# FFN steps of a two-network kernel: two weight blocks of a pair split by one operation per engine

## The reference, cut to what matters

```
def swiglu(h, w1, w3, w2):
    return (jax.nn.silu(h @ w1) * (h @ w3)) @ w2

x = x + 0.5 * m[:, 0, 2][:, None] * swiglu(adaln_in(x, norm_g[l, 0], m, 0),
                                           ffn_w1[l, 0], ffn_w3[l, 0], ffn_w2[l, 0])
```

## Time and profile before

| | |
|---|---|
| median of 3 runs | 1666.9 us (1659.82 to 1667.51) |
| profiled execution | 1665.64 us |
| its span, first to last instruction | 1663.8 us |
| PE busy | 1467.2 us (88%) |
| DVE busy | 1384.0 us (83%) |
| ACT busy | 985.6 us (59%) |
| mean granted TensorE clock | 0.942 of full |

### The profile page before, as it was taken

The page is one execution under the profiler, slowest core; times in us unless marked ns, Lnnn a source line. Parts: engine busy times, 40 slices in busy tenths (PEclk is TensorE's granted clock), DMA queues, the critical chain, the costliest instruction groups (busy, mean ns, idle before and its releaser), DMA issues.

```text
span 1663.8 us, 27728 instructions
## 1 busy us (share of the span) xinstructions
PE 1467.2 (88%) x11160; PEld 1392.3 (84%) x11160; DVE 1384.0 (83%) x2275; ACT 985.6 (59%) x1643; POOL 79.3 (5%) x152
## 2 busy tenths in 40 slices
PE   5897786798978887988899999899999999988997
PEld 4897775687978886867899999888899899868997
DVE  7597957799999998886888988796788888787986
ACT  4354554565566455654666766556666766676765
POOL 0012110001110110000000000000000000000000
PEclk9698988999999999999999999898999999999999
DMA  9499945569986996426697787444677677534783
GB/s 384 150 406 351 411 152 190 214 226 361 353 308 226 402 404 260 139 90 267 218 322 270 244 278 275 143 150 152 250 280 276 232 267 271 210 115 185 275 274 127
DMA packets 84973, 420.30 MB, mean 253 GB/s; under 512 B 9364, under 2 KB 9796, under 8 KB 58095
## 3 DMA queue, kind: packets, MB, share of 16 engines
q1 hardware_dynamic: 64478, 343.48, 56.9%
q0 software_dynamic: 20368, 75.06, 11.9%
HBM read 417.37 MB, written 1.13 MB: 252 GB/s over the span
## 4 chain that ended last, share of the span: by engine, by line
PE 42%; DVE 7%; ACT 2%; issue 1%; DVEq 0%
PE pw L628 14%; PE pw L629 13%; PE acc L628 6%; PE acc L629 6%; DVE low_p L1965 2%; DVE low_d L1965 1%; PE acc L938 1%; PE pw L896 1%; DVE h_lo L1818 1%; DVE x L2012 0%; PE acc L918 0%; ACT hi_p L1453 0%; ACT h_hi L1363 0%; DVE prob L2154 0%; DVE KR L2154 0%
## 5 line engine op out<-in xcount | busy, mean ns | idle before, releaser
L628 PE MATMUL pw<-h_hi,hi_p 128*128 128x256 f32 x2928 | 740.8, 291 | 38.1 <-DVE low_p L1965 28.0
L629 PE MATMUL pw<-h_lo,low_p 128*128 128x256 f32 x2928 | 729.7, 288 | 0.0
L628 PEld LDWEIGHTS pw<-h_hi,hi_p 128*128 128x128 f32 x2928 | 576.0, 197 | 58.7 <-DVE low_p L1965 28.9
L629 PEld LDWEIGHTS pw<-h_lo,low_p 128*128 128x128 f32 x2928 | 576.5, 197 | 0.4 <-issue 0.2
L1965 DVE SCALAR_TENSOR_TENSOR low_p<-hi_p,land_p 128x1024 fp32r<-128x1024 f32 x418 | 507.6, 1222 | 44.7 <-ACT hi_p L1453 44.5
L1453 ACT ACTIVATE hi_p<-land_p 128x1024 fp32r<-128x1024 f32 x418 | 434.4, 1048 | 74.4 <-DMA land_p<-stream 74.4
L628 PE MATMUL acc<-a_hi,hi_d 128*128 128x256 f32 x1376 | 354.5, 293 | 66.3 <-DVE low_d L1965 60.0
L629 PE MATMUL acc<-a_lo,low_d 128*128 128x256 f32 x1376 | 350.5, 291 | 0.0
L628 PEld LDWEIGHTS acc<-a_hi,hi_d 128*128 128x128 f32 x1376 | 274.1, 199 | 74.1 <-issue 67.5
L629 PEld LDWEIGHTS acc<-a_lo,low_d 128*128 128x128 f32 x1376 | 274.7, 200 | 0.0
L1965 DVE SCALAR_TENSOR_TENSOR low_d<-hi_d,land_d 128x1024 fp32r<-128x1024 f32 x205 | 249.7, 1219 | 5.9 <-ACT hi_d L1453 5.8
(11 more groups left out here) (356 smaller groups left out, 1757.7 us busy)
## 6 DMA issues: line engine op xcount, KB each, us to landing
land_p<-stream SPq DMA_DIRECT2D x207, 1024.0 KB, 5.1
land_d<-stream SPq DMA_DIRECT2D x209, 512.0 KB, 5.5
modw<-wmod POOLq DMA_DIRECT2D x116, 512.0 KB, 8.3
biasT<-wmod POOLq DMA_DIRECT2D x12, 512.0 KB, 4.8
biasT<-bias_rows POOLq DMA_DIRECT2D x3, 1536.0 KB, 10.6
modw<-wmod SPq DMA_DIRECT2D x8, 512.0 KB, 11.2
biasT<-wmod SPq DMA_DIRECT2D x8, 512.0 KB, 14.6
biasT<-bias_rows POOLq DMA_DIRECT2D x1, 3072.0 KB, 13.5
```

The source lines that it names most:

```text
L628: mm(o, lhs[0], rhs[0], start=start, stop=False, skip_group_check=True)
L629: return mm(o, lhs[1], rhs[1], start=False, stop=stop, skip_group_check=True)
```

## The change

In the FFN steps the two blocks of a pair are split by one operation per engine, over both blocks (128 x 2048), where there were two operations of 128 x 1024. On ACT both now come after `a_hi`, followed by the third block. On DVE the low part of step j-1's third block moves behind the gate, to where block 0's low part was, and the low part of the pair comes after `a_lo`. DVE uses the wide operation in smooth steps only, ACT in all steps. Where the pair has one block, or lies behind the end of the stream, the old operations are used.

```diff
@@ ACT
+            def pair_high(group):
+
+                if len(group) < 2 or group[0][0] >= NT:
+                    split_high(group)
+                    return
+                t = group[0][0]
+                assert SPLITS[high[0]:high[0] + 2] == group
+                high[0] += 2
+                act.wait_ge(land_load[t % NPAIR], 16 * (t // NPAIR + 1))
+                fn(hi_p[:, t % NPAIR], land_p[:, t % NPAIR], ACT.Copy, scale=1.0 / TWICE).then_inc(hi_ready, 2)
+
...
-                between = STEPS[i, j][0:1] if smooth(i, j) else []
-                split_high(between)
                 act.wait_ge(gated_ready, f * NFF + j + 1)
                 fn(a_hi[0:r, j % (LAG + 1), :], act_in[0:r, j % 2, :], ACT.Copy, scale=ONCE).then_inc(a_hi_ready, 1)
                 if i == j == 0:
                     hidden_plain(range(KD))
                 if j or not (deferred(i) or i in RAW):
-                    split_high(STEPS[i, j][len(between):])
+                    pair_high(STEPS[i, j][:-1])
+                    split_high(STEPS[i, j][-1:])
@@ DVE
+            def pair_low(group):
+
+                if len(group) < 2 or group[0][0] >= NT:
+                    split_low(group)
+                    return
+                t = group[0][0]
+                assert SPLITS[low[0]:low[0] + 2] == group
+                low[0] += 2
+                dve.wait_ge(hi_ready, SPLIT_NO[t, 1])
+                v.scalar_tensor_tensor(low_p[:, t % NPAIR], hi_p[:, t % NPAIR], -ONCE, land_p[:, t % NPAIR], ALU.mult, ALU.add).then_inc(lo_ready, 2)
+
...
-                    if smooth(i, j) and smooth(i, j - 1):
-                        split_low(STEPS[i, j - 1][-1:])
                     dve.wait_ge(silu_done, f0 + j + 1)
...
                     v.tensor_tensor(act_in[0:r, j % 2, :], sig[0:r, j % 2, :], up_half, ALU.mult).then_inc(gated_ready, 1)
-                    if smooth(i, j):
-                        split_low(STEPS[i, j][0:1])
+                    if smooth(i, j) and smooth(i, j - 1):
+                        split_low(STEPS[i, j - 1][-1:])
                     dve.wait_ge(a_hi_ready, f0 + j + 1)
...
                     if smooth(i, j):
-                        split_low(STEPS[i, j][1:-1])
+                        pair_low(STEPS[i, j][:-1])
```

## The result

The changed kernel takes 1763.82 us (median of 4 runs, 1760.63 to 1767.33); the kernel before took 1667.2 beside it (1659.82 to 1668.12). The ratio is 1.059, with a 95% interval of 1.0553 to 1.0627. The forecast was 1750, in a range of 1727 to 1780. The profiled execution of after took 1767.33 us; against the span of before its span is 101.7 us longer, where the working had added 84.3.

The account below looks back on a forecast made before the run. The prediction took DVE to bound FFNs 0, 2 and 3 and PE the late ones; a closed chain would set longer steps. Stage losses summed to 84.3 us, so 1665.6 + 84.3 = 1750 us, range 1727 to 1780.

Parts of the forecast that it names:

- The closed chain: Gate, a_hi, pair's high part, low part: 4.90 us in FFNs 0, 2, 3; with scaled and silu 6.08 in late FFNs.
- The step: FFNs 0, 2, 3 with two modulation blocks: 7.20 us against 6.42; FFNs 6, 8, 9, 11: 6.08 against 5.76.
- ACT's saving is worth nothing by itself: Wide high part on ACT takes 1.88 us against 1.99 for two; no gain, as ACT is never the bound.
- By stage: Added us: FFN 0 10, FFN 2 13.7, FFN 3 15.8, FFN 5 2, FFNs 6, 8, 9 35.1 together, FFN 11 7.7.
- FFN 0: Adds 13.3 us in 17 steps, 1 in steps 1 and 2, 1.9 at the end, less 6 given back: 10.
- land earlier relative to their use: Transfers: SP's order unchanged and loads start on PE's progress, so they come earlier relative to use; no size given.
- FFN 5: Mean step of 5.4 us stays below PE's 5.76, so only the ends cost: 2 us.
- A: Rival: PE stays at 5.76 us per step in FFNs 6, 8, 9, 11; 1727 us in all; chance 0.06.
- B: Rival: PE's clock falls from 0.95 to 0.86 in three FFNs, 10 us each; 1780 us; chance 0.10.
- C: Rival: pair's high part is ready when DVE comes, only the 0.08 us saving counts; 1662 us; chance 0.02.
- D: Rival: the change doesn't do what it says in the 157 steps; given no chance of its own.
- the bounds of 1740 and 1772: Lower: FFN 0 gets back all 9.4 us, durations 0.05 shorter; upper: wide operations take 1.99 and 2.36 us.

Follow-up runs that it names:

- The first experiment: Changed kernel's order on both engines, but each pair split by two 1024-column operations instead of one of 2048; 1672.12 us, ratio 1.0043.
- e6_first_ffns: The change in FFNs 0, 2, 3 and 5 only, FFNs 6, 8, 9 and 11 as in the kernel before; 1714.96 us, ratio 1.0296.
- e8_flat_low: Changed kernel with the wide low part written over one flat row of 2048 columns instead of 2 x 1024; 1765.19 us, ratio 1.0597.
- e1_narrow: The first experiment: the changed kernel's order with 1024-column operations on both engines; 1672.12 us.
- e7_mixed: Kernel before, with wide operations in steps 3 to 19 of FFNs 0, 2, 3 only, high part ahead of the gate wait; 1667.62 us, ratio 1.0005.

## Why the prediction was right, point by point

**The mechanism: right.** The closed chain from the gate over `a_hi` and the pair's high part to its low part sets the step in FFNs 0, 2 and 3, and scaled and silu join it in FFNs 6, 8, 9 and 11. The kernel with the same order and narrow operations shows that the width makes the chain this long (1672 against 1764), and the one with ACT in the old order that ACT's order is needed for it too (1686). The Trainium skill (Perfetto Trace Analysis, Optimizing Scalar/DVE Operations) ties breaking instructions up to Scalar and Vector engines that aren't saturated but cause bubbles on others, a condition that the prediction left out. The first experiment agrees: in the changed kernel DVE was busy for 78% of the span. Of the same section's sentence that grouping can improve throughput if the engine is saturated, the runs show 0.08 us per step where no engine waits, and nothing in the kernel's time.

**The step.** 7.27 to 7.28 against 7.20, and 6.16 to 6.17 against 6.08. Two terms were small: the handover 0.10 instead of 0.04, and the wide high part 1.90 instead of 1.88. The wide low part was right at 2.29, with the next instruction after 2.21. The sentence that ACT's saving is worth nothing by itself doesn't fit this chain, which ACT's operation is part of: with ACT narrow the kernel took 9.6 us more. 0.08 over 17 + 14 + 18 + 60 + 19 = 128 steps is 10 us of the 17.4 by which the sum fell short.

**By stage,** by the updates of x at the end of each. FFN 2 lost 14.7 (13.7 predicted), FFN 3 14.1 (15.8), FFN 6 14.2, FFN 8 13.6 and FFN 9 13.5 (11.7 each), FFN 11 10.9 (7.7). In FFNs 6, 8 and 9 the longer steps are most of the difference, 1.6 us in each; in FFN 6 one step also took 6.92, since PE had waited 3.29 us and then ran at the lower of its two levels (granted clock 0.50 from 988 to 992 us). In FFN 11 they are half of 3.2: the interval to scaled of step 21 was 4.28 and not 3.84, and the end took 0.8 more, where I had it give back 0.5. In FFN 3 two errors went against each other, for the step was longer than I said and the sum still smaller: of the 19 intervals between its gates, twelve grew by 0.82 to 0.86 and the other seven by -0.99 to +0.62, 10.99 in all, where I had counted 18 equal ones. Among the seven are steps that had held waits of their own before (8.62 us, now 8.43) and the one with the half slice (6.46, now 5.47).

**FFN 0,** 13.8 instead of 10. I let 6 of the 9.4 us of waits for modulation weights be given back. The waits for them between 50 and 700 us in the changed kernel are a single one, in FFN 0 (us in total, times, longest):

```profile
DVE modw L1807 <- DMA modw<-wmod: 6.4, 1, 6.4
```

The step of the long wait took 14.00 us instead of 16.43, so about 3 came back. Another 2 came back in the step of 8.43 before, 7.27 now, which had waited for a pair to land. So 5 of the 6 were given back. The rest of the 3.8 is in the steps, 7.27 and not 7.20, and in steps 1 and 2, which cost 0.85 each where I had 1 for both. The trace shows what stands ahead of these loads on POOL: a wait for the transfer of a table (`par_s`) of 11.14 us, 12.32 before. SP starts that transfer at 125.73 us instead of 117.03, since it stands on a queue that goes by PE's progress. I had treated that queue as a gain only ("land earlier relative to their use").

**FFN 5,** 6.7 to 7.6 instead of 2 (6.7 in `e6_first_ffns` and 6.6 in `e8_flat_low`): the step of the prediction that failed. I compared the mean step, 5.4, with PE's 5.76. But steps with no modulation block take 4.98 now, those with one 6.13 to 6.14, and a mean hides that the long ones are over PE's pace while the short ones can't go ahead of it. Before, steps of 4.13 to 4.14 made good what long ones had cost. From `a_lo` of step 2 to that of step 21 it took 105.3 us before and 109.2 after; 2.5 more are the end's. This is read from the two traces; no run tests it by itself.

**The mixers,** where I said nothing would change: +2.8 in the first, -0.7, -1.6 and -0.75 in the others. The first one took 113.6 us before and 116.3 after, but 111.8 in the kernel with the change in the early FFNs and 111.7 in the one without it there. So it moves by some us from one profile to the next, and the +2.8 is not shown to be the change's.

**The rivals.** A (late FFNs stay at 5.76) fell: scaled comes every 6.16, with no wait for PE in the steady state. B (the clock falls to 0.86 in FFNs 2 and 3) fell: 0.91 and 0.97 there, 0.92 in FFN 0, and 0.936 over the whole against 0.942. Only FFN 2 went down, from 0.95, and its undisturbed steps kept the 7.27 to 7.28 of the chain. C (faster) fell at its own point: the high part takes 1.90, not 1.04. D can be excluded: 157 wide low parts are in the trace. The time lies between the bounds of 1740 and 1772, 13.8 us above the forecast.

## What to carry to other kernels

Before an operation is made wider, look whether another engine takes its result up piece by piece, or makes its input so: then the consumer's start moves by the length of the piece, here 0.93 us for 0.08 saved, and most of it counts as soon as both engines' queues close into a loop. Add up that loop for each kind of step, and not for the mean step: a stage is as slow as its long steps if the short ones can't catch up. A chain just under the bound's pace (5.66 against 5.76) looks free and still cost 2.4 to 5.1 us a stage, because the old one (4.73) had been used to catch up at its start.

## What the chip showed that I had not expected

A low part of 2048 columns that had waited started 0.09 to 0.11 us after the end of the high part that released it (151 of 153 in the changed kernel; the other two 0.46), one of 1024 columns 0.03 (`e1_narrow`: 1001.46 + 1.04 to 1002.53). It is so behind a wide and behind a narrow high part, and with flat operands; a narrow low part behind a wide high part shows 0.03 to 0.04 too. When the wide one has nothing to wait for, it is not to be seen. Timeline of DVE in FFN 3 of the kernel that keeps the gain (`e7_mixed`):

```profile
598.14 0.42 DVE L2133 SCALAR_TENSOR_TENSOR a_lo<-gu,a_hi 128x256 fp32r<-128x256 f32 x1
598.48 2.29 DVE L1994 SCALAR_TENSOR_TENSOR low_p<-hi_p,land_p 128x2048 fp32r<-128x2048 f32 x1
600.68 1.23 DVE L1815 SCALAR_TENSOR_TENSOR modw<-modw,condb 128x1024 f32<-128x1024 f32 x1
```

Here 0.34 us lie between the starts of `a_lo` and the wide one, no more than between the gate and the narrow `low_d` (649.35 to 649.68 in the changed kernel). Why a longer operation takes longer to start after a wait stays open.
